# A hybrid decoder layer in fp32 precision: 1056 tokens cut into 512, 512 and 32 instead of three times 352

## The reference, cut to what matters

```python
ada = (c @ w_ada + b_ada)          # shift1, scale1, gate1, shift2, scale2, gate2, one set for each sequence
h = rmsnorm(x, g_norm1) * (1.0 + scale1) + shift1
z = h @ w_in                       # q, k, v, gates of two mixers (mLSTM and GLA), 1024 -> about 8200 columns
...                                # short convolution, mLSTM over chunks, GLA over chunks, states out
y = (sigmoid(g_a) * ha + sigmoid(g_b) * hb) @ w_out
x = x + gate1 * y
h2 = rmsnorm(x, g_norm2) * (1.0 + scale2) + shift2
x = x + gate2 * ((silu(h2 @ w_ffn_gate) * (h2 @ w_ffn_up)) @ w_ffn_down)     # 1024 -> 2816 -> 1024
```

## Time and profile before

| | |
|---|---|
| median of 2 runs | 2217.39 us (2212.11 to 2222.68) |
| profiled execution | 2215.02 us, its span 2213.3 us |
| TensorE matmuls busy | 2076.8 us (94%) |
| TensorE weight loads busy | 1959.7 us (89%) |
| VectorE, ScalarE, PoolE busy | 820.0, 570.4, 596.0 us |
| mean granted TensorE clock | 0.96 of full |

### The profile page before, as it was taken

How to read it: one execution, slowest core, us unless ns; L and a number is a source line. 1 busy time by engine, 2 the same in 40 slices (tenths; PEclk the granted TensorE clock), 3 DMA queues, 4 the chain that set the end, 5 groups by cost and what they waited for, 6 DMA issues and landing times. The chain is left out here.

```text
span 2213.3 us, 33045 instructions
## 1 busy us (share of the span) xinstructions
PE 2076.8 (94%) x12501; PEld 1959.7 (89%) x12501; DVE 820.0 (37%) x1494; ACT 570.4 (26%) x1164; POOL 596.0 (27%) x481
## 2 busy tenths in 40 slices
PE   7699999999999999999998889499999999999997
PEld 3689999898898898988998789399999999999997
DVE  4541264311553205524036332613323333233326
ACT  3332324222333223331333220211121112111122
POOL 3221132211231212312112065332332233222330
PEclk9799999999999899998998989799999999999999
DMA  8221221222221212213123151011111111111111
GB/s 269 84 63 48 66 71 39 72 72 70 63 53 51 88 52 77 56 35 104 42 60 103 56 180 39 10 48 48 49 40 48 49 48 47 41 48 49 48 49 79
DMA packets 193052, 144.52 MB, mean 65 GB/s; under 512 B 9396, under 2 KB 178548, under 8 KB 191872
## 3 DMA queue, kind: packets, MB, share of 16 engines
q1 hardware_dynamic: 192896, 142.32, 21.3%
HBM read 119.75 MB, written 22.54 MB: 64 GB/s over the span
## 5 line engine op out<-in xcount | busy, mean ns | idle before, releaser
L1091 POOL TENSOR_TENSOR w_lo<-w_raw,w_hi 128x512 fp32r<-128x512 f32 x130 | 179.3, 1379 | 839.0 <-ACT w_hi L932 830.8
L775 PE MATMUL bank<-h_hi,w_hi 128*128 128x352 f32 x1560 | 346.3, 345 | 26.2 <-ACT w_hi L932 18.1
L775 PE MATMUL bank<-h_lo,w_hi 128*128 128x352 f32 x1560 | 324.3, 331 | 0.0
L775 PE MATMUL bank<-h_hi,w_lo 128*128 128x352 f32 x1560 | 322.0, 329 | 0.0
L1804 POOL TENSOR_TENSOR f_lo<-w_raw,f_hi 128x512 fp32r<-128x512 f32 x148 | 190.1, 1304 | 427.0 <-ACT f_hi L1735 426.8
L775 PEld LDWEIGHTS bank<-h_hi,w_hi 128*128 128x128 f32 x1560 | 266.2, 196 | 43.3 <-issue 19.5
L1656 PE MATMUL bank<-h_hi,f_hi 128*128 128x352 f32 x1248 | 254.7, 327 | 32.5 <-issue 16.8
L775 PEld LDWEIGHTS bank<-h_lo,w_hi 128*128 128x128 f32 x1560 | 271.8, 195 | 0.0
L775 PEld LDWEIGHTS bank<-h_hi,w_lo 128*128 128x128 f32 x1560 | 269.1, 193 | 0.1
L1656 PE MATMUL bank<-h_lo,f_hi 128*128 128x352 f32 x1248 | 253.4, 325 | 4.4 <-POOL h_lo L1845 3.3
L1656 PE MATMUL bank<-h_hi,f_lo 128*128 128x352 f32 x1248 | 252.2, 324 | 0.0
(11 more groups left out here) (332 smaller groups left out, 2389.0 us busy)
## 6 DMA issues: line engine op xcount, KB each, us to landing
w_raw<-in_w_in SPq DMA_DIRECT2D x128, 256.0 KB, 2.8
w_ada_tile<-in_w_ada SPq DMA_DIRECT2D x32, 512.0 KB, 3.9
w_raw<-in_w_ffn_gate SPq DMA_DIRECT2D x44, 256.0 KB, 3.0
w_raw<-in_w_ffn_up SPq DMA_DIRECT2D x44, 256.0 KB, 2.9
w_raw<-in_w_ffn_down SPq DMA_DIRECT2D x44, 256.0 KB, 2.7
w_ada_ring<-in_w_ada SPq DMA_DIRECT2D x8, 1024.0 KB, 5.5
x_scratch<-x_turned_rows SPq DMA_DIRECT2D x1, 4224.0 KB, 13.0
x_t<-x_scratch SPq DMA_DIRECT2D x4, 1056.0 KB, 12.7
```

What stands on the lines that cost most here:

```text
L775: last = pe.matmul(g.ps[b][:, 0:n], x[:, s, k, :], y[:, 4 * h + k, c0:c0 + n], start=(h == 0 and k == 0 and m == 0), stop=(h == 1 and k == ...
L1091: pool.tensor_tensor(Wl[:, s], raw[:, r], Wh[:, s].bitcast(F32), ALU.subtract).then_inc(s_lo, 1)
```

## The change

The pieces become columns 0 to 511, 512 to 1023 and 1024 to 1055: the first two hold prompt tokens alone and fill a PSUM bank each, the third holds the samples alone. Both `span` functions return these. What follows from it:

- `evacuate` has no prompt part in the third piece (`if cut`).
- For out and down the third piece needs `samples` alone, which reads columns 0 to 31 of its bank and sets the bank free itself, with a nop on VectorE behind the wait for its first operation; `add_prompt` runs for the first two pieces only, on all their columns.
- PoolE's `squares` and TensorE's final transposes wait for the samples' counter (s_stm) instead of the third piece's bank.

The number of matmuls, their order, the weight tiles and the DMAs stay as they are.

```diff
--- before.py
+++ after.py
@@ -31,7 +31,6 @@
 TAU = 16.0
 BIG = 1e30
 NPC = 3
-PC = T // NPC
 NCOND = 1 + NSEQ
 ZP = SEQ + W4 - 1
 ZS = SLEN + W4 - 1
@@ -632,7 +631,7 @@
             return i * (2 * per) + (first + (per if isB(w) else 0))
 
         def span(c):
-            return c * PC, PC
+            return c * P * 4, (P * 4, P * 4, NS)[c]
 
         def wait_piece(e, w, i, l, c):
 
@@ -950,7 +949,8 @@
                         if c == 0:
                             nth = (0 if w == "S" else i * 2 + 2) + (1 if name == "k" else 0)
                             wait(act, s_silu, nth)
-                        last = act.activation(Z[:, W4 - 1 + c0:W4 - 1 + c0 + cut], src[:, 0:cut], ACT.Copy)
+                        if cut:
+                            last = act.activation(Z[:, W4 - 1 + c0:W4 - 1 + c0 + cut], src[:, 0:cut], ACT.Copy)
                         if last_c:
                             z = Z[:, ZP:ZN].rearrange("p (b t) -> p b t", t=ZS)[:, :, W4 - 1:ZS]
                             last = act.activation(z, src[:, cut:n].rearrange("p (b t) -> p b t", t=SLEN), ACT.Copy)
@@ -1714,9 +1714,7 @@
                 pe.transpose(MISC[2][0:H * NCOND, 0:P], g.nout[:, :], g.ident[:, :]).then_inc(s_co, 1)
                 run(pe, step)
 
-                lastp = Place(LOOP, None, 0)
-                bnk, turns = lastp.piece(23)
-                pe.wait_ge(s_pf[bnk], turns + 1)
+                pe.wait_ge(s_stm, 2 * KC * (1 + NBLK))
                 for t in range(NT):
                     n = P if t < NC else NS
                     for b in range(2):
@@ -1805,8 +1803,7 @@
 
                 def squares(n):
 
-                    bnk, turns = out_place(n).piece(2)
-                    pool.wait_ge(s_pf[bnk], turns + 1)
+                    pool.wait_ge(s_stm, 2 * (n + 1))
                     if n == 0:
                         pool.tensor_tensor(SQ[:, :], X[:, 0, :], X[:, 0, :], ALU.mult).then_inc(s_sq, 1)
                     else:
@@ -1857,7 +1854,8 @@
                         for c in range(NPC):
                             if c == NPC - 1:
                                 samples("out", pl, c, b, 2 * KC, b + 1)
-                            add_prompt("out", pl, c, b, c, 2 * KC)
+                            else:
+                                add_prompt("out", pl, c, b, c, 2 * KC)
                     elif kind == "norm2":
                         dve.wait_ge(s_stm, 2 * KC)
                         bnk, turns = out_place(KC - 1).piece(NPC - 1)
@@ -1911,14 +1909,14 @@
                             n, c = 4 * (k // 12) + k % 12 // 3, k % 3
                             if c == NPC - 1:
                                 samples("down", pl, k, n, 5 * KC, b * KC + (KC + n + 1))
-                            add_prompt("down", pl, k, n, c, 5 * KC)
+                            else:
+                                add_prompt("down", pl, k, n, c, 5 * KC)
 
                 def add_prompt(kind, pl, k, n, c, vec):
                     wait_full(dve, kind, pl, k)
                     bnk, _ = pl.piece(k)
                     c0, w = span(c)
-                    m = min(w, SEQ - c0)
-                    dve.scalar_tensor_tensor(X[:, n, c0:c0 + m], g.ps[bnk][:, 0:m], g.ada[:, vec + n, 0:1], X[:, n, c0:c0 + m],
+                    dve.scalar_tensor_tensor(X[:, n, c0:c0 + w], g.ps[bnk][:, 0:w], g.ada[:, vec + n, 0:1], X[:, n, c0:c0 + w],
                                              ALU.mult, ALU.add).then_inc(s_pf[bnk], 1)
 
                 def samples(kind, pl, k, n, vec, count):
@@ -1926,9 +1924,10 @@
                     wait_full(dve, kind, pl, k)
                     bnk, _ = pl.piece(k)
                     wait(dve, s_stm, count * 2 - 2)
-                    dve.tensor_tensor(seqv(stm[:, :]), seqv(g.ps[bnk][:, PC - NS:PC]), bc(g.ada[:, vec + n, 1:NCOND].unsqueeze(2), SLEN),
+                    dve.tensor_tensor(seqv(stm[:, :]), seqv(g.ps[bnk][:, 0:NS]), bc(g.ada[:, vec + n, 1:NCOND].unsqueeze(2), SLEN),
                                       ALU.mult).then_inc(s_stm, 1)
                     dve.wait_ge(s_stm, count * 2 - 1)
+                    dve.nop(nofuse=True).then_inc(s_pf[bnk], 1)
                     dve.tensor_tensor(X[:, n, SEQ:T], X[:, n, SEQ:T], stm[:, :], ALU.add).then_inc(s_stm, 1)
 
                 def rows_out(t):
```

## The result

| | before | after |
|---|---|---|
| median | 2217.39 us | 2521.64 us (2517.43 and 2525.84) |
| ratio | 1 | 1.137, 95% interval 1.123 to 1.151 |
| span of the profiled execution | 2213.3 us | 2515.7 us |
| mixer phase, first to last L775 (L774) | 1181.6 us | 1316.3 us |
| behind it | 955.7 us | 1119.9 us |

The change makes the kernel 13.7% slower; 2500 us were forecast, in a range of 2395 to 2560. The span grew by 302.4 us: 134.7 in the mixer phase, 164.2 behind it, 3.5 ahead of it.

A forecast was written before the change was run, and what follows sets the result against it. TensorE's own matmul stream was taken as the bound: 2215.0 us + 287 for the 3336 sets + 7 for the clock - 10 for closed waits = 2499, given as 2500 us, range 2395 to 2560.

The forecast's parts named there:

- What bounds the kernel: Almost everywhere TensorE's own stream ends last (busy 94%), so the cost of one matmul there decides, 160 ns at 352 columns.
- Price of a small one: A 32-column matmul in the third piece costs 112 ns, set by its weight load; bounds 27 and 224 ns.
- The two signs: F32R load recorded at 196 ns against 198 at L921; first F32R matmul behind L921 sat 0.09 us for its weights.
- Price of a large one: A 512-column matmul costs 227 ns: 213 of columns and the fixed 13 extra of the 352s; ends 215 and 233.
- One set: Two large matmuls and one small take 566 ns against 480 for three of 352, +86 ns; times 3336, +287 us.
- Correction (a): Mixer work at 1.2 GHz: a set goes from 879 to 1078 ns there; for some 65 sets +7 us.
- Correction (b): In the mixer, longer pieces close part of TensorE's up to 35 us of waits: -10 us, bounds 0 and 35.
- The other engines at nothing: VectorE's 778 ns add, ScalarE's evacuation, moved waits and DMAs stay covered by TensorE's pieces; set at nothing.
- The nearly free small piece: Every small piece: loads pulled ahead, 27 ns per small matmul; 2138 us (4%), or no change with 227 ns large ones (3%).
- the load at 56 ns: Small matmuls' F32R weight load takes one cycle a column, 56 ns: a set 510 ns, +100 us, 2315 us; 6%.
- the narrow matmul in two passes: 32-column F32R matmuls run as two passes or slower, 224 ns: a set 678 ns, +660 us, 2875 us; 5%.
- The clock rival: Clock falls in the big loops too: a quarter of the sets at 1.2 GHz, +427 us on top, 2925 us; 4%.

## Why the prediction was right

- **What bounds the kernel** held: TensorE's own spacing. In the FFN blocks no other engine, bank or wait came into the chain.
- **Price of a small one, 112 ns.** Measured 112. The two signs that an F32R load costs as much as a plain fp32 one (its length, and the 0.09 us behind L921) were right, and the experiments with 64 weight columns and with 96 and 224 token columns show that it follows the load's columns and not its own.
- **Price of a large one, 227 ns.** This term was too small: 230. The step that failed is the reason for it, that the extra is something each weight load does to the stream, once for each matmul. Half the load left 161 ns at 352 columns. The widths show mostly a slope instead: 352 take 160 and 512 take 230, 0.4375 ns a column and some 6 ns for each matmul, which gave 516 ns for the sets of 448 (measured 518) and 480 for those of 400 (482). The line misses single widths by up to 2 ns (448: 204 ns), so it is a fit and not a law. The right value lay within the ends of 215 and 233.
- **One set, +86 ns**: measured 572 - 480 = +92, so 307 us instead of 287. Here lie the missing 20 us.
- **Correction (a), +7 us for the clock**, took the low time as given. It grew: the mean clock in the mixer went from 0.96 to 0.95, the time at 1.2 GHz from 87 to 134 us. **Correction (b), -10 us of closed waits**: 39.8 us fell to 15.7, -24. For the mixer 1560 x 92 ns = 143.5, less 24.1, leaves 119.4; the phase grew by 134.7, and the remainder of some 15 us is put down to the clock (argued, not measured apart). Both corrections were too small, by 8 and 14 us with opposite signs, so most of that cancelled by luck. Another 3.5 us came ahead of the mixer, which no term had.
- **The FFN phase**: 1776 x 92 ns = 163.4 us, measured 164.2.
- **The other engines at nothing** held: 751 ns for the add, no idle time before L1684.
- **The rivals.** The nearly free small piece, the load at 56 ns and the narrow matmul in two passes fall with the spacing of 112. The clock rival was wrong for the FFN loop, where the clock stayed at 1.00, and had a small part of truth in the mixer, 15 us in the change and some 25 that 224 columns won back. The gap of N/2.4 + 2.5 ns with a floor of 25 ns in the Trainium skill ("TensorE: Matmul & The Clock Gate", section "Back-to-back issue gap") would have made this change a gain; the same section calls it the gap of an isolated matmul and says that for narrow ones it leaves out the weight load. Here, where each matmul brings its own weights, the spacings were 230 ns against its 216 and 112 against its 25.

## What to carry to other kernels

Where each matmul brings its own 128 weight columns in F32R, count it as the longer of its stream and its load; here, at 2.4 GHz, the load was 112 ns, the stream 6 ns and 0.44 for each column, and by this fit they cross at some 243 columns (224 took 112 ns, 256 took 118). Cut the moving dimension so that no piece falls under that point, and cut it evenly if in doubt: three even pieces of 352 took 480 ns a set, 400, 400 and 256 took 482, two full banks and a rest 572. A leftover piece wasn't hidden by putting it between large ones, but it could stream 224 columns for the price of 32. A price for each instruction should be read from the distance between starts in a run of equals: the recorded lengths (263 ns for a small matmul, 192 for its load) are no price.

## What was not expected of the hardware

- The stream of F32R at 2.4 GHz took 0.4375 ns a column between 352 and 512 columns (a column a cycle would be 0.417) and lost nothing at 1.2 GHz (293 ns for 352). Halving the load beside it changed nothing (161 ns against 160).
- Filling the small pieces from 32 to 224 columns of the same 112 ns raised the mean granted clock of the mixer from 0.95 to 0.98 and took 25 us off; 96 columns didn't. Why is open.
- Four executions with the same code in the mixer differed by up to 20 us there (1310.7 to 1330.6), with mean clocks of 0.95 and 0.94 and 125 to 169 us at 1.2 GHz. Why is open, too.
